# Local attention in one block of 128 scores a head: a predicated fold, a fused maximum and masked parts behind the denominators

## The chip, the cores and the metric

One core of a Trainium2 chip. The metric is the device time of one execution in microseconds (us); the runs shown are medians of three.

The engines: TensorE (PE; its weight loads are PEld), VectorE (DVE), ScalarE (ACT), GpSimd (POOL), SyncE (SP), which here issues the transfers.

## The reference

A decoder block on x (1, 2048, 1024), float32: RMS norm, one input projection, two groups of heads side by side (a gated linear recurrence and sliding-window attention), one output projection, and a SwiGLU network. The change touches the attention:

```python
scores = einsum('bnqhgd,bnshd->bnhgqs', qb, kk) * (B_HEAD_DIM ** -0.5)
dist = qi + BLOCK - kj                       # BLOCK = 128; kj runs over 2 * BLOCK keys: the block before and its own
valid = ((dist >= 0) & (dist < WINDOW))[None] & (key_pos >= 0)[:, None, :]    # WINDOW = 128
scores = scores - slopes[:, :, None, None] * dist
scores = where(valid, scores, -inf)
m = maximum(max(scores, axis=-1), sink)
p = exp(scores - m)
p = p / (sum(p, axis=-1) + exp(sink - m))
o = einsum('bnhgqs,bnshd->bnqhgd', p, vv)
```

There are 8 heads of 64, with 2 heads of keys and values. A query at place q of its block sees the keys q+1 to 127 of the block before and the keys 0 to q of its own: always 128 keys, and each place 0 to 127 is taken exactly once over the two blocks.

## The kernel before

**Blocks and slots.** The 2048 tokens are four blocks of 512 (the loop `for it in range(NSB)`). A block goes through 27 slots. In slots 0 to 21 TensorE makes one group of 128 columns of the input projection (`group`, L940: 24 matmuls, since each f32 product is three of rounded high and low parts), in the later ones parts of the output projection. Between these groups the same slot holds the small steps of attention and of the recurrence, each step of one turn further along. Each engine has its own program with its own loop over the slots, in order, and the engines meet at semaphores. After the four blocks come the two halves of the SwiGLU network (`ffn`, `down`), which the change doesn't touch.

**The weight parts.** For each group, SyncE loads the raw weights, ScalarE makes the high part (`make_hi`, L1251, once the group of the same slot is done), and VectorE the low part (`make_lo`, L1697), two slots ahead of use.

**A turn of attention.** A turn is one pair of heads and 128 queries: 16 turns in a block, 64 in all. The constants SCORE, PROBS, P_TURN and PV (2, 3, 4, 5) say how many slots behind the turn's number a step stands:

- slot i+2: TensorE makes the scores, 256 a head, in bank X[0] (`scores`, L987). VectorE adds the position term from `dist` (or `dist0` where there is no block before), with a large negative number in masked places (L1749, one operation a head), takes the maximum (L1753) and makes two small terms with the sink (L1756, L1760). ScalarE takes the exponentials with their sums (L1332) and that of the sink (L1334).
- slot i+3: VectorE adds up the denominators and takes reciprocals (`denominators`, L1730 and L1734), the first thing in its slot; GpSimd multiplies the probabilities by them (`normalise`, L2300).
- slot i+4: TensorE transposes the four 128x128 parts of `pr` into bank X[1] (`p_turn`, L1010), which must have been read for the turn before (`s_pT`); ScalarE copies the bank to `pT` (`p_turn`, L1340).
- slot i+5: TensorE multiplies by the values, over both blocks of keys (`pv`, L1021).

In VectorE's slot there follow, behind the denominators: `make_lo`, the gate of the recurrence, the low part of the queries (L1884), the scores of turn slot-2, every fourth slot a copy of the outputs (L1892), the recurrence of a head (L1767 to L1793), its mask (L1802), its state update (L1820, eight operations in a row) and its norm (L1828), and the scaling of the block before (L2023). In TensorE's slot the order is group, transposes of the recurrence, scores, `p_turn`, `pv`, and the recurrence's products.

Of the kernel before, what the change touches and what calls it, by code (L numbers as in the profile page):

```python
# [33 lines left out]
F32 = mybir.dt.float32  # L34
# [6 lines left out]
P = 128  # L41
# [86 lines left out]


def step_at(slot, first):  # L130

    return slot - first if 0 <= slot - first < STEPS else None


def block_program(nc, x, ln1_g, w_in, lb_logits, hgrn_norm_g, attn_sinks, attn_norm_g, w_out, ln2_g,
# [37 lines left out]
    with ExitStack() as ctx:  # L173
# [52 lines left out]
        gu = [at(f"gu{i}", (P, T), gu_at + 2 * K * i) for i in range(2)]  # L226
        dist = at("dist", (P, 2 * BLOCK), dist_at)
        dist0 = at("dist0", (P, 2 * BLOCK), dist_at + K)
        causal = at("causal", (P, P), dist_at + 2 * K)
# [190 lines left out]
        s_mx = sem("s_mx")  # L420
        s_nm = sem("s_nm")
        s_nms = sem("s_nms")
        s_exp = sem("s_exp")
        s_den = sem("s_den")
        s_rd = sem("s_rd")
        s_prob = sem("s_prob")
# [12 lines left out]
        s_yblo = sem("s_yblo")  # L439
        s_dist = sem("s_dist")  # L440

# [71 lines left out]

        INI, DST = 10, 4

# [375 lines left out]
        def _(pe):  # L891
# [355 lines left out]
        def _(act):  # L1247
# [147 lines left out]
            def slots(it):  # L1395
                for slot in range(SLOTS):
# [23 lines left out]
                    if slot in Q_SLOT:  # L1420
# [22 lines left out]
                    if slot == SWA_MUL:  # L1443
                        swa_hi(it, 0)
                    for begin, step in ((P_TURN, p_turn), (SCORE, scores), (PV, pv)):
                        i = step_at(slot, begin)
# [225 lines left out]
        def _(dve):  # L1672
            V = nc.vector

            def parameters():
# [18 lines left out]
                V.tensor_copy(causal[:, :].bitcast(I32), causal[:, :]).then_inc(s_ini2, 1)  # L1694
                dve.wait_ge(s_ini2, 11)

# [30 lines left out]
            def denominators(it, i):  # L1727
                w = i % 2
                dve.wait_ge(s_exp, it * STEPS + i + 1)
                V.tensor_tensor(den[:, :], rs[:, w, :], es[:, :], ALU.add).then_inc(s_den, 1)  # L1730
                dve.wait_ge(s_den, it * STEPS + i + 1)
                if i:
                    dve.wait_ge(s_prob, it * STEPS + i)
                V.reciprocal(rd[:, :], den[:, :]).then_inc(s_rd, 1)  # L1734

            def scores(it, i):
# [3 lines left out]
                if i >= 2:  # L1740
                    dve.wait_ge(s_ptr, it * STEPS + i - 1)
                if i == 0 and it:
                    dve.wait_ge(s_dist, it)
                d = dist0 if b == 0 else dist
                for par in range(2):

                    slope = 2.0 ** -(2 * p + par + 1)
                    half = slice(par * 256, (par + 1) * 256)
# [6 lines left out]
                dve.wait_ge(s_mx, it * STEPS + i + 1)  # L1755
                V.scalar_tensor_tensor(out=nm[:, w, :], in0=mx[:, :], scalar=-0.125,  # L1756
                                       in1=nsinks[:, 2 * p:2 * p + 2], op0=ALU.mult,
                                       op1=ALU.min).then_inc(s_nm, 1)
                dve.wait_ge(s_nm, it * STEPS + i + 1)
# [98 lines left out]
            def slots(it):  # L1858
                for slot in range(SLOTS):
                    i = step_at(slot, PROBS)  # L1860
                    if i is not None:
                        denominators(it, i)
                    mul = head_at(slot, NORM_MUL)
                    n = unit_made_at(slot)
# [14 lines left out]
                    if slot in Q_SLOT:  # L1879
                        p = Q_SLOT.index(slot)  # L1880
                        dve.wait_ge(s_qhi, it * PAIRS + p + 1)
                        for par in range(2):
                            rows, others = slice(64 * par, 64 * par + 64), slice(64 - 64 * par, 128 - 64 * par)
                            V.tensor_tensor(qs[p % 2][par][others, :], bank[rows, :],  # L1884
                                            qs[p % 2][par][rows, :].bitcast(F32), ALU.subtract).then_inc(s_q, 1)
# [353 lines left out]
        def _(pool):  # L2239
# [12 lines left out]

            G.iota(dist[:, :].bitcast(I32), [[1, 2 * BLOCK]], base=-BLOCK, channel_multiplier=-1).then_inc(s_ini, 1)
# [4 lines left out]
            G.tensor_copy(dist0[:, :], dist[:, :].bitcast(I32)).then_inc(s_ini, 1)  # L2258
            pool.wait_ge(s_ini, 9)

            G.memset(causal[0:CHUNK, CHUNK:P], 0.0).then_inc(s_ini, 1)

            G.affine_select(out=dist0[:, :], in_=dist0[:, :], compare_op=ALU.is_ge, fill=MASKED, base=BLOCK,
                            pattern=[[-1, 2 * BLOCK]], channel_multiplier=1).then_inc(s_dst, 1)
            pool.wait_ge(s_dst, 1)
            G.affine_select(out=dist[:, :], in_=dist0[:, :], compare_op=ALU.is_ge, fill=MASKED, base=-1,
                            pattern=[[1, 2 * BLOCK]], channel_multiplier=-1).then_inc(s_dst, 1)
            pool.wait_ge(s_dst, 2)
            G.tensor_copy(dist0[:, BLOCK:2 * BLOCK], dist[:, BLOCK:2 * BLOCK]).then_inc(s_dst, 1)
            G.memset(dist0[:, 0:BLOCK], MASKED).then_inc(s_dst, 1)  # L2270
            pool.wait_ge(s_dst, 4)
            pool.wait_ge(s_ini, 10)

# [22 lines left out]
            def normalise(it, i):  # L2296

                pool.wait_ge(s_rd, it * STEPS + i + 1)
                halves = pr[i % 2][:, :].rearrange("p (h k) -> p h k", h=2)
                G.tensor_tensor(halves, halves, rd[:, :].rearrange("p (h o) -> p h o", o=1)  # L2300
                                .broadcast_to([P, 2, 2 * BLOCK]), ALU.mult).then_inc(s_prob, 1)
                if i == (PAIRS - 1) * TB + 1:

                    pool.wait_ge(s_bias, it * STEPS + i)
                    copy(dist0[:, :], dist[:, :]).then_inc(s_dist, 1)

# [99 lines left out]
```

## Time and profile before

| | |
|---|---|
| median of 3 runs | 2208.97 us (2208.25 to 2210.03) |
| the profiled execution | 2210.06 us |
| its span, first to last instruction | 2208.3 us |
| granted TensorE clock, mean | 0.996 |

In the profile's rows, L12 is a line of the kernel; a group is line, engine, operation, output<-inputs by the program's names, count, then busy us, mean ns of one and the idle time of its engine ahead of it with what ended it. Busy time is a union: overlapping instructions count once. Matmuls overlap, so the mean of one is longer than its share. Durations and starts are those of the profiled execution, whose time stands 1.1 us above the median.

### The profile page before, as it was taken

The page shows a single profiled execution, that of the slowest core. Times are in us where ns is not written, and L with a number is a line of the kernel's source. Part 1 is how long each engine was busy: PE and PEld are TensorE (multiplying, and loading weights), DVE is VectorE, ACT ScalarE, POOL GpSimd, SP SyncE. Part 2 cuts the span into 40 slices and gives each one's busy share as a digit, 9 for nine tenths or more (in the row PEclk, how much of TensorE's full clock was granted, in tenths as well). Part 3 has the DMA queues.
Part 4 walks back from the last instruction along what each step waited for, and adds up shares of the span by engine and source line. Part 5 has one row for each costly group of instructions (what it writes and reads, how often), then busy time and mean ns, then how long its engine had stood idle before and what let it go on. Part 6 is the DMA issues. An engine that isn't in the chain of part 4 may idle for free.

```text
span 2208.3 us, 29312 instructions
## 1 busy us (share of the span) xinstructions
PE 2163.4 (98%) x10792; PEld 1788.8 (81%) x10792; DVE 1427.8 (65%) x2126; ACT 972.9 (44%) x1775; POOL 473.4 (21%) x377
## 2 busy tenths in 40 slices
PE   7999999999999999999999999999999999999997
PEld 6887888888888888778888887887888888887886
DVE  5776678657865786857466675568665556454555
ACT  5444454446444644443433333346533333333444
POOL 1342024202320232232232330000223232210000
PEclk9999999999999999999999999999999999999999
DMA  4232332343235324543446566887432323227765
GB/s 125 86 125 68 124 96 87 115 144 104 77 101 166 97 68 139 176 143 121 128 167 220 196 228 210 256 270 253 160 119 90 119 96 119 92 97 238 224 209 214
DMA packets 261534, 323.86 MB, mean 147 GB/s; under 512 B 16400, under 2 KB 167952, under 8 KB 261392
## 3 DMA queue, kind: packets, MB, share of 16 engines
q1 hardware_dynamic: 261392, 321.98, 44.2%
q8 instruction: 87, 1.43, 0.3%
q14 instruction: 55, 0.45, 0.1%
HBM read 244.85 MB, written 77.07 MB: 146 GB/s over the span
## 4 chain that ended last, share of the span: by engine, by line
PE 79%; issue 9%; DVE 5%; POOL 3%; DMA 2%; ACT 1%; SPq 0%; DVEq 0%; POOLq 0%; ACTq 0%
PE M L1194 10%; PE M L1196 10%; PE M L1195 10%; PE M L896 5%; PE M L898 5%; PE M L897 5%; PE M L1220 3%; PE M L1221 3%; PE M L1222 3%; PE X L1196 3%; PE X L1194 3%; PE X L1195 3%; PE X L1220 3%; PE X L1222 3%; PE X L1221 3%
## 5 line engine op out<-in xcount | busy, mean ns | idle before, releaser
L2155 DVE TENSOR_TENSOR ring_lo<-ring_raw,ring_hi 128x1024 fp32r<-128x1024 f32 x154 | 190.6, 1238 | 169.4 <-ACT ring_hi L1604 169.2
L896 PE MATMUL M<-uhi,whi 128*128 128x512 f32 (+1 forms) x720 | 286.1, 397 | 3.7 <-DVE wlo L1701 2.1
L1701 DVE TENSOR_TENSOR wlo<-raw,whi 128x1024 fp32r<-128x1024 f32 x120 | 162.2, 1351 | 196.7 <-ACT whi L1255 196.2
L898 PE MATMUL M<-uhi,wlo 128*128 128x512 f32 (+1 forms) x720 | 278.9, 387 | 0.0
L897 PE MATMUL M<-ulo,whi 128*128 128x512 f32 (+1 forms) x720 | 278.6, 387 | 0.0
L1604 ACT ACTIVATE ring_hi<-ring_raw 128x1024 fp32r<-128x1024 f32 x154 | 163.3, 1061 | 234.6 <-DMA ring_raw<-a_scr 231.1
L1194 PE MATMUL M<-t_hi,wu_hi 128*128 128x512 f32 x616 | 240.7, 391 | 4.4 <-DVE gq L2073 2.6
L1196 PE MATMUL M<-t_hi,wu_lo 128*128 128x512 f32 x616 | 240.4, 390 | 0.0
L1195 PE MATMUL M<-t_lo,wu_hi 128*128 128x512 f32 x616 | 240.1, 390 | 0.0
L1255 ACT ACTIVATE whi<-raw 128x1024 fp32r<-128x1024 f32 x120 | 126.8, 1056 | 207.1 <-PE M L898 129.5
L2041 DVE TENSOR_TENSOR wu_lo<-fraw,wu_hi 128x512 fp32r<-128x512 f32 x132 | 124.9, 955 | 122.5 <-ACT wu_hi L1544 122.1
L2300 POOL TENSOR_TENSOR pr<-pr,rd 128x512 f32<-128x512 f32 x64 | 88.6, 1384 | 459.0 <-DVE rd L1734 459.0
L896 PEld LDWEIGHTS M<-uhi,whi 128*128 128x128 f32 x720 | 136.7, 190 | 35.9 <-issue 7.8
L2369 POOL TENSOR_TENSOR fs<-fraw 128x512 f32<-128x512 f32 x44 | 63.1, 1435 | 456.8 <-DMA fraw<-in_w_gate_dram 210.6
L898 PEld LDWEIGHTS M<-uhi,wlo 128*128 128x128 f32 x720 | 136.5, 190 | 28.1
L897 PEld LDWEIGHTS M<-ulo,whi 128*128 128x128 f32 x720 | 136.8, 190 | 24.4
L1194 PEld LDWEIGHTS M<-t_hi,wu_hi 128*128 128x128 f32 x616 | 115.8, 188 | 29.5 <-DVE wu_lo L2041 4.3
L2375 POOL TENSOR_TENSOR fraw<-fraw,fs 128x512 f32<-128x512 f32 x44 | 58.6, 1332 | 363.2 <-DVE wl_lo L2041 363.2
L1195 PEld LDWEIGHTS M<-t_lo,wu_hi 128*128 128x128 f32 x616 | 116.1, 188 | 24.2
L1196 PEld LDWEIGHTS M<-t_hi,wu_lo 128*128 128x128 f32 x616 | 115.9, 188 | 24.2
L1332 ACT ACTIVATE pr<-pr,nm 128x256 f32<-128x256 f32 x128 | 64.2, 502 | 151.3 <-DVE nms L1760 151.3
L1220 PE MATMUL M<-ring_hi 128*128 128x512 f32 x308 | 120.9, 393 | 4.4 <-DVE ring_lo L2155 4.4
(275 smaller groups left out, 4954.2 us busy)
## 6 DMA issues: line engine op xcount, KB each, us to landing
raw<-in_w_in_dram SPq DMA_DIRECT2D x88, 512.0 KB, 3.9
ring_raw<-a_scr SPq DMA_DIRECT2D x154, 256.0 KB, 3.7
fraw<-in_w_gate_dram SPq DMA_DIRECT2D x44, 512.0 KB, 4.5
fraw<-in_w_up_dram SPq DMA_DIRECT2D x44, 512.0 KB, 4.8
a_scr<-au SPq DMA_DIRECT2D x88, 256.0 KB, 2.4
ring_raw<-t_scr SPq DMA_DIRECT2D x88, 256.0 KB, 3.0
ring_raw<-in_w_down_dram SPq DMA_DIRECT2D x66, 256.0 KB, 3.0
raw<-in_w_out_dram SPq DMA_DIRECT2D x32, 512.0 KB, 3.9
```

The costliest lines, as they stand in the source:

```text
L896: mm(bank, whi[s][:, kb, :], hi, start=first, stop=False)
L897: mm(bank, whi[s][:, kb, :], lo, start=False, stop=False)
L898: return mm(bank, wlo[s][:, kb, :], hi, start=False, stop=last)
L1194: mm(bank[:, :], wh[:, k, :], hi[:, k, :], start=start and k == 0, stop=False, skip_group_check=True)
L1195: mm(bank[:, :], wh[:, k, :], lo[:, k, :], start=False, stop=False, skip_group_check=True)
L1196: last = mm(bank[:, :], wl[:, k, :], hi[:, k, :], start=False, stop=k == KH - 1, skip_group_check=True)
L1220: mm(banks[b][:, :], hi[:, 1, tokens], hi[:, 0, :], start=first, stop=False, skip_group_check=True)
L1221: mm(banks[b][:, :], hi[:, 1, tokens], lo[:, 0, :], start=False, stop=False, skip_group_check=True)
L1222: done = mm(banks[b][:, :], lo[:, 1, tokens], hi[:, 0, :], start=False, stop=last, skip_group_check=True)
L1604: A(hi[:, :, :], raw_r[:, :, :], ACT.Copy).then_inc(s_rowhi, 1)
L1701: V.tensor_tensor(wlo[s][:, :, :], raw[s][:, :, :], whi[s][:, :, :].bitcast(F32), ALU.subtract).then_inc(s_lo[s], 1)
L2155: V.tensor_tensor(lo[:, :, :], raw_r[:, :, :], hi[:, :, :].bitcast(F32), ALU.subtract).then_inc(s_rowlo, 1)
```

## The change

- The scores of a head are folded from 256 to 128 in the bank itself: a predicated copy writes the scores of the own block (places up to q) over those of the block before. The queries are scaled on the way in by 0.125 divided by the head's slope, so that one table `dist` of 128 serves for both blocks.
- One operation a head adds the table, scales and takes the maximum; it takes the place of the addition and the separate maximum. For the first 128 tokens `dist0` has the negative number in the missing places.
- Exponentials and the product with the reciprocals cover 128 a head.
- TensorE transposes two parts a turn in place of four. The two parts (block before, own block) are made by masking with AND as the bank is copied: `p_parts`, on VectorE, in slot i+5 behind the denominators, instead of ScalarE's copy in slot i+4. The product with the values is as before, with its parts in another order.
- GpSimd's set-up makes the new tables; the copy of `dist` once a block goes.

```diff
         dist = at("dist", (P, BLOCK), dist_at)
         dist0 = at("dist0", (P, BLOCK), mix_at + 22 * K)
         upto_row = at("upto_row", (P, BLOCK), dist_at + 512)
         parts = at("parts", (P, 2, BLOCK), dist_at + K)
...
# TensorE, p_turn
-                for n in range(4):
+                for n in range(2):
                     last = tr(X[1][:, n * P:(n + 1) * P], pr[i % 2][:, n * P:(n + 1) * P], ident[:, :])
# TensorE, pv
-                                  pT[i % 2][:, (2 * par + kb) * P:(2 * par + kb + 1) * P],
+                                  pT[i % 2][:, (2 * kb + par) * P:(2 * kb + par + 1) * P],
...
# ScalarE, scores and p_turn
-                    act.wait_ge(s_den, it * STEPS + i)
+                    act.wait_ge(s_den, 2 * (it * STEPS + i) - 1)
                 for par in range(2):
-                    half = pr[w][:, par * 256:(par + 1) * 256]
+                    half = pr[w][:, par * BLOCK:(par + 1) * BLOCK]
...
-            def p_turn(it, i):
-                act.wait_ge(s_ptr, it * STEPS + i + 1)
-                if i >= 2:
-                    act.wait_ge(s_pv, it * STEPS + i - 1)
-                A(pT[i % 2][:, :], X[1][:, :], ACT.Copy).then_inc(s_pT, 1)
...
-                            last = A(qs[p % 2][par][rows, :], bank[rows, :], ACT.Copy)
+                            last = A(qs[p % 2][par][rows, :], bank[rows, :], ACT.Copy, scale=0.125 / slope_of(p, par))
...
# VectorE, scores
-                d = dist0 if b == 0 else dist
+                d = dist0 if it == 0 and b == 0 else dist
+                both = X[0][:, :].rearrange("p (h k) -> p h k", h=2)
+                V.copy_predicated(both[:, :, 0:BLOCK],
+                                  upto_row[:, :].bitcast(I32).rearrange("p (o k) -> p o k", o=1)
+                                  .broadcast_to([P, 2, BLOCK]), both[:, :, BLOCK:2 * BLOCK]).then_inc(s_fold, 1)
+                dve.wait_ge(s_fold, it * STEPS + i + 1)
                 for par in range(2):
-                    last = V.scalar_tensor_tensor(out=pr[w][:, half], in0=d[:, :], scalar=8.0 * slope,
-                                                  in1=X[0][:, half], op0=ALU.mult, op1=ALU.add)
+                    last = V.tensor_tensor_reduce(pr[w][:, par * BLOCK:(par + 1) * BLOCK], both[:, par, 0:BLOCK],
+                                                  d[:, :], 8.0 * slope_of(p, par), MASKED, ALU.add, ALU.max,
+                                                  mx[:, par:par + 1])
                 last.then_inc(s_bias, 1)
                 dve.wait_ge(s_bias, it * STEPS + i + 1)
-                V.tensor_reduce(mx[:, :], pr[w][:, :].rearrange("p (h k) -> p h k", h=2), AX_X,
-                                ALU.max).then_inc(s_mx, 1)
...
+            def p_parts(it, i):
+                dve.wait_ge(s_ptr, it * STEPS + i + 1)
+                if i >= 2:
+                    dve.wait_ge(s_pv, it * STEPS + i - 1)
+                V.tensor_tensor(pT[i % 2][:, :].rearrange("p (k h q) -> p k h q", k=2, h=2).bitcast(I32),
+                                X[1][:, 0:2 * P].rearrange("p (o h q) -> p o h q", o=1, h=2).bitcast(I32)
+                                .broadcast_to([P, 2, 2, P]),
+                                parts[:, :, :].rearrange("p k (o q) -> p k o q", o=1).bitcast(I32)
+                                .broadcast_to([P, 2, 2, P]), ALU.bitwise_and).then_inc(s_pT, 1)
...
# VectorE, slots
                     if i is not None:
                         denominators(it, i)
+                    i = step_at(slot, PV)
+                    if i is not None:
+                        p_parts(it, i)
...
# GpSimd, normalise
-                halves = pr[i % 2][:, :].rearrange("p (h k) -> p h k", h=2)
+                halves = pr[i % 2][:, 0:2 * BLOCK].rearrange("p (h k) -> p h k", h=2)
```

Left out of the diff: the set-up of the tables on GpSimd (some ten small operations in place of six), one cast of `parts` on VectorE, and the low part of the queries, which gets the same scale (`scalar_tensor_tensor` in place of `tensor_tensor`, same shape).

## Rows read from the trace of the kernel before

**Rows 1.** The page's first part: busy us, share, instructions, by engine.

```profile
PE 2163.4 (98%) x10792; PEld 1788.8 (81%) x10792; DVE 1427.8 (65%) x2126; ACT 972.9 (44%) x1775; POOL 473.4 (21%) x377
```

**Rows 2.** Windows: first and second block's attention; length, busy by engine, PEclk, DMA, GB/s.

```profile
39.00:182.00 143.00, 142.37 (x868) 117.79 (x870) 104.82 (x228) 67.38 (x174) 43.02 (x37) 1.00 0.31 100
262.00:406.00 144.00, 142.81 (x876) 117.86 (x874) 110.01 (x232) 76.82 (x188) 42.92 (x37) 1.00 0.29 90
```

**Rows 3.** Groups by line: busy us, mean ns | idle before, releaser.

```profile
L1010 PE MATMUL X<-ident,pr 128*128 128x128 f32 x256 | 38.3, 272 | 0.0
...
L1749 DVE SCALAR_TENSOR_TENSOR pr<-dist,X 128x256 f32<-128x256 f32 x128 | 47.6, 412 | 0.5
L1753 DVE TENSOR_REDUCE mx<-pr 128x2 f32<-128x512 f32 x64 | 43.9, 686 | 2.2
L1820 DVE SCALAR_TENSOR_TENSOR st<-st,cum,X 128x128 f32<-128x128 f32 x112 | 39.0, 348 | 4.0
...
L1802 DVE TENSOR_TENSOR amask<-X,causal 128x512 int32<-128x512 int32 x16 | 10.9, 680 | 0.0
...
L1340 ACT ACTIVATE pT<-X 128x512 f32<-128x512 f32 x64 | 37.8, 590 | 0.2
...
L1332 ACT ACTIVATION_READ_ACCUMULATOR pr<-pr,nm 128x1 f32 x128 | 23.9, 187 | 0.0
...
L2300 POOL TENSOR_TENSOR pr<-pr,rd 128x512 f32<-128x512 f32 x64 | 88.6, 1384 | 459.0 <-DVE rd L1734 459.0
```

**Rows 4.** Timeline of TensorE, second block, turns 1, 5, 7, 10, 11, 12, 15: start, us.

```profile
280.42 0.60 PE L1010 MATMUL X<-ident,pr 128*128 128x128 f32 x4
...
312.03 0.60 PE L1010 MATMUL X<-ident,pr 128*128 128x128 f32 x4
...
329.00 0.60 PE L1010 MATMUL X<-ident,pr 128*128 128x128 f32 x4
...
353.42 0.60 PE L1010 MATMUL X<-ident,pr 128*128 128x128 f32 x4
...
363.81 0.60 PE L1010 MATMUL X<-ident,pr 128*128 128x128 f32 x4
...
371.04 0.60 PE L1010 MATMUL X<-ident,pr 128*128 128x128 f32 x4
...
395.76 0.60 PE L1010 MATMUL X<-ident,pr 128*128 128x128 f32 x4
```

**Rows 5.** Timeline of VectorE, same stretch: reciprocals of turns 2, 6, 8, 11, 12, 13, last update.

```profile
281.05 0.17 DVE L1734 RECIPROCAL rd<-den 128x2 f32<-128x2 f32 x1
...
313.33 0.17 DVE L1734 RECIPROCAL rd<-den 128x2 f32<-128x2 f32 x1
...
329.49 0.17 DVE L1734 RECIPROCAL rd<-den 128x2 f32<-128x2 f32 x1
...
355.36 0.17 DVE L1734 RECIPROCAL rd<-den 128x2 f32<-128x2 f32 x1
...
364.08 0.17 DVE L1734 RECIPROCAL rd<-den 128x2 f32<-128x2 f32 x1
...
372.64 0.17 DVE L1734 RECIPROCAL rd<-den 128x2 f32<-128x2 f32 x1
...
392.95 2.65 DVE L1820 SCALAR_TENSOR_TENSOR st<-st,cum,X 128x128 f32<-128x128 f32 x7
```

**Rows 6.** Timeline of ScalarE and VectorE: the weight parts made ahead of turn 12.

```profile
362.42 1.06 ACT L1255 ACTIVATE whi<-raw 128x1024 fp32r<-128x1024 f32 x1 [1.75 <-PE M L898]
...
364.16 1.22 DVE L1701 TENSOR_TENSOR wlo<-raw,whi 128x1024 fp32r<-128x1024 f32 x1
```

**Rows 7.** Waits of TensorE: who waited for whom, us in total, times, longest.

```profile
PE M L1194 <- DVE gq L2073: 2.6, 1, 2.6
```

**Rows 8.** Windows of the columns of rows 2, in the SwiGLU part.

```profile
942.60:946.00 3.40, 3.40 (x10) 2.63 (x9) 0.18 (x1) 0.59 (x2) 1.00 (x1) 0.50 1.02 337
946.00:949.40 3.40, 3.40 (x16) 2.80 (x15) 0.69 (x1) 1.92 (x5) 0.00 (x0) 0.99 0.61 243
```

More of the change, by code:

```diff
@@ L127, in head_at, with slope_of @@
     return F_SLOT.index(slot - offset) if slot - offset in F_SLOT else None
+def slope_of(p, par):
+    return 2.0 ** -(2 * p + par + 1)
 def step_at(slot, first):
@@ L226, in block_program @@
         gu = [at(f"gu{i}", (P, T), gu_at + 2 * K * i) for i in range(2)]
-        dist = at("dist", (P, 2 * BLOCK), dist_at)
-        dist0 = at("dist0", (P, 2 * BLOCK), dist_at + K)
+        dist = at("dist", (P, BLOCK), dist_at)
+        dist0 = at("dist0", (P, BLOCK), mix_at + 22 * K)
+        upto_row = at("upto_row", (P, BLOCK), dist_at + 512)
+        parts = at("parts", (P, 2, BLOCK), dist_at + K)
         causal = at("causal", (P, P), dist_at + 2 * K)
@@ L420, in block_program @@
         s_mx = sem("s_mx")
-        s_nm = sem("s_nm")
+        s_fold = sem("s_fold")
         s_nms = sem("s_nms")
@@ L1444, in slots @@
                         swa_hi(it, 0)
-                    for begin, step in ((P_TURN, p_turn), (SCORE, scores), (PV, pv)):
+                    for begin, step in ((SCORE, scores), (PV, pv)):
                         i = step_at(slot, begin)
@@ L1694, in parameters @@
                 V.tensor_copy(causal[:, :].bitcast(I32), causal[:, :]).then_inc(s_ini2, 1)
-                dve.wait_ge(s_ini2, 11)
+                V.tensor_copy(parts[:, :, :].bitcast(I32), parts[:, :, :]).then_inc(s_ini2, 1)
+                dve.wait_ge(s_ini2, 12)
             def make_lo(it, n):
@@ L1730, in denominators @@
                 V.tensor_tensor(den[:, :], rs[:, w, :], es[:, :], ALU.add).then_inc(s_den, 1)
-                dve.wait_ge(s_den, it * STEPS + i + 1)
+                dve.wait_ge(s_den, 2 * (it * STEPS + i) + 1)
                 if i:
                     dve.wait_ge(s_prob, it * STEPS + i)
-                V.reciprocal(rd[:, :], den[:, :]).then_inc(s_rd, 1)
+                V.reciprocal(rd[:, :], den[:, :]).then_inc(s_den, 1)
             def scores(it, i):
@@ L1883, in slots @@
                             rows, others = slice(64 * par, 64 * par + 64), slice(64 - 64 * par, 128 - 64 * par)
-                            V.tensor_tensor(qs[p % 2][par][others, :], bank[rows, :],
-                                            qs[p % 2][par][rows, :].bitcast(F32), ALU.subtract).then_inc(s_q, 1)
+                            V.scalar_tensor_tensor(out=qs[p % 2][par][others, :], in0=bank[rows, :],
+                                                   scalar=0.125 / slope_of(p, par),
+                                                   in1=qs[p % 2][par][rows, :].bitcast(F32),
+                                                   op0=ALU.mult, op1=ALU.subtract).then_inc(s_q, 1)
                     i = step_at(slot, SCORE)
@@ L2265, in _ @@
-            pool.wait_ge(s_dst, 1)
-            G.affine_select(out=dist[:, :], in_=dist0[:, :], compare_op=ALU.is_ge, fill=MASKED, base=-1,
-                            pattern=[[1, 2 * BLOCK]], channel_multiplier=-1).then_inc(s_dst, 1)
+            G.iota(upto_row[:, :].bitcast(I32), [[1, BLOCK]], base=-BLOCK, channel_multiplier=-1).then_inc(s_ini, 1)
+            pool.wait_ge(s_ini, 11)
+            G.affine_select(out=dist0[:, :], in_=dist[:, :], compare_op=ALU.is_ge, fill=0.0, base=0,
+                            pattern=[[-1, BLOCK]], channel_multiplier=1).then_inc(s_dst, 1)
@@ L2268, in _ @@
+            G.tensor_copy(parts[:, 1, :], upto_row[:, :].bitcast(I32)).then_inc(s_dst, 1)
             pool.wait_ge(s_dst, 2)
-            G.tensor_copy(dist0[:, BLOCK:2 * BLOCK], dist[:, BLOCK:2 * BLOCK]).then_inc(s_dst, 1)
-            G.memset(dist0[:, 0:BLOCK], MASKED).then_inc(s_dst, 1)
+            G.affine_select(out=parts[:, 1, :], in_=parts[:, 1, :], compare_op=ALU.is_ge, fill=0.0, base=-1,
+                            pattern=[[1, BLOCK]], channel_multiplier=-1).then_inc(s_dst, 1)
+            pool.wait_ge(s_dst, 3)
@@ L2271, in _ @@
+            G.tensor_tensor(dist[:, :], dist0[:, :], parts[:, 1, :], ALU.add).then_inc(s_dst, 1)
             pool.wait_ge(s_dst, 4)
-            pool.wait_ge(s_ini, 10)
+            G.memset(upto_row[:, :], -1.0).then_inc(s_dst, 1)
+            G.memset(parts[:, :, :], -1.0).then_inc(s_dst, 1)
+            G.affine_select(out=dist0[:, :], in_=dist[:, :], compare_op=ALU.is_ge, fill=MASKED, base=0,
+                            pattern=[[-1, BLOCK]], channel_multiplier=1).then_inc(s_dst, 1)
+            pool.wait_ge(s_dst, 7)
@@ new lines, in _ @@
+            G.affine_select(out=upto_row[:, :], in_=upto_row[:, :], compare_op=ALU.is_ge, fill=0.0, base=0,
+                            pattern=[[-1, BLOCK]], channel_multiplier=1).then_inc(s_dst, 1)
+            G.affine_select(out=parts[:, 0, :], in_=parts[:, 0, :], compare_op=ALU.is_ge, fill=0.0, base=-1,
+                            pattern=[[-1, BLOCK]], channel_multiplier=1).then_inc(s_dst, 1)
+            G.affine_select(out=parts[:, 1, :], in_=parts[:, 1, :], compare_op=ALU.is_ge, fill=0.0, base=0,
+                            pattern=[[1, BLOCK]], channel_multiplier=-1).then_inc(s_dst, 1)
@@ L2274, in copy @@
+            pool.wait_ge(s_dst, 10)
             def copy(out, in_):
@@ L2296, in normalise @@
             def normalise(it, i):
-                pool.wait_ge(s_rd, it * STEPS + i + 1)
-                halves = pr[i % 2][:, :].rearrange("p (h k) -> p h k", h=2)
+                pool.wait_ge(s_den, 2 * (it * STEPS + i) + 2)
+                halves = pr[i % 2][:, 0:2 * BLOCK].rearrange("p (h k) -> p h k", h=2)
                 G.tensor_tensor(halves, halves, rd[:, :].rearrange("p (h o) -> p h o", o=1)
[L2301 to L2305, printed above, removed]
+                                .broadcast_to([P, 2, BLOCK]), ALU.mult).then_inc(s_prob, 1)
             def add_squares(it, p):
```

19 lines of the change are left out of this document (5 added, 14 removed).

## The prediction

> **What bounds the kernel now.** I read the busy shares first: TensorE is busy for 98% of the span, VectorE for 65%, ScalarE for 44% [rows 1]. The reader should see that only TensorE is full, so a change pays where it takes work from TensorE and costs where it makes TensorE wait. Then the stretches in which attention runs, one for each block of 512 tokens: in the first TensorE is busy 142.4 of 143 us, in the second 142.8 of 144, and the third and fourth repeat the second within 0.1 us. VectorE is busy 105 and 110 us there, three quarters of the time and far more than its mean [rows 2]. So attention now costs TensorE no waits to speak of, but VectorE is the engine with the least room. Third, the groups of the instructions that the change touches [rows 3], and last the timeline of both engines, turn by turn [rows 4, 5].
>
> A turn i (0 to 15 in a block) is spread over slots: its scores are made in slot i+2, its denominators come at the head of VectorE's slot i+3, TensorE transposes its probabilities in slot i+4 and multiplies by the values in slot i+5. The transposes of turn i share one bank, X[1], with those of turn i-1, and so wait until these are copied out.
>
> **Part 1, two transposes fewer.** Four transposes of 272 ns each [rows 3] take 0.60 us together [rows 4], so they start (0.60 - 0.272) / 3 = 0.109 us apart. Two are left. That is 2 x 0.109 = 0.22 us a turn, 64 turns: 14.0 us of TensorE time, all of it on the path, since TensorE waits for nothing there. The Trainium skill's page TensorE: Matmul & The Clock Gate (section Back-to-back issue gap) has about 81 ns for a sustained 128-column matmul, which would make this 64 x 2 x 0.081 = 10.4 us; the trace's f32 transposes are slower, and the sum goes by the trace.
>
> **Part 2, the copy moves from ScalarE to VectorE, and one slot later.** Now ScalarE copies the bank in 0.59 us [rows 3] in the slot of the transposes, a whole slot before the next ones want it. The changed code makes it an AND of 512 elements on VectorE, at the head of VectorE's next slot, behind the denominators. The nearest row is the causal AND of 128x512 from PSUM, 0.68 us [rows 3]. So the transposes of turn i now wait for this chain: VectorE finishes everything of its slot i+3, makes the sum and reciprocal of turn i+1, then the AND for turn i-1. What is queued behind the wait on TensorE is everything: it runs in order. A VectorE instruction starts 0.09 us before the end shown for the one ahead of it (the reciprocal at 364.08 ends at 364.25, the next starts at 364.16 [rows 5, 6]), and I add 0.06 us for the signal: transposes can start 0.09 less, 0.68 + 0.06 more, so 0.65 us after the reciprocal's end.
>
> Now the reader should set the reciprocal of turn i+1 [rows 5] against the transposes of turn i [rows 4]. In the second block the reciprocal ends after the transposes have started in these turns: turn 1, 281.22 against 280.42, late by 0.80; turn 5, 313.50 against 312.03, 1.47; turn 7, 329.66 against 329.00, 0.66; turn 10, 355.53 against 353.42, 2.11; turn 11, 364.25 against 363.81, 0.44; turn 12, 372.81 against 371.04, 1.77. Today that costs nothing, for nobody on TensorE waits for it. In turn 15 no reciprocal comes ahead, but the state update of VectorE's slot ends at 395.60 and the transposes start at 395.76.
>
> **Part 3, less work in the scores on VectorE.** Gone: two operations of 128x256 at 0.41 us (about 0.74 for the pair, since they overlap) and a maximum over 512 at 0.69 [rows 3]; with the gaps 1.49 us up to the next operation. Added: a predicated copy of 128x256 and two fused operations of 128x128 that also give the maximum. No row shows either form. The copy I take at the 0.41 of a 128x256 operation from PSUM, with the gap 0.45. A 128x128 operation from PSUM is the state update, 0.35 [rows 3]; two that overlap are 0.54, and for writing out the maximum I add 0.1 each, from ScalarE's accumulator read of 0.187 that half overlaps [rows 3]. Together 1.2, a saving of 0.3 us a turn. Bounds: with nothing for the maximum and a cheaper copy, 0.8, saving 0.7; if each of the three takes what 512 elements take, 0.68, it is 2.0, a loss of 0.5. I take 0.3, since the 128x128 row is nearest in size and source. On the maximum the Trainium skill's page VectorE: DVE Perf Modes (Two Vector instructions with no wait between them) says that an operation which also writes out its accumulator is two instructions; no row of VectorE here shows one. With two operations as short as the reciprocal's 0.17 us, unhidden, the saving would be 0.16, and the waits below some 3 us more.
>
> **Part 4, the rest.** ScalarE loses its copy and half of each exponential's elements: it waits for VectorE anyway, so nothing, except that it gives back 0.2 us at turn 1. GpSimd's product goes from 512 to 256 elements (1.38 us for 512 [rows 3]); it runs in the slot ahead of its transposes and waits for VectorE's reciprocal, so nothing. The scaled query copies have the same shapes. The set-up is longer by some small operations on GpSimd and one cast on VectorE, all ahead of the first turn and beside TensorE's first groups: nothing. No DMA is added or moved.
>
> **The sum.** A turn waits for its lateness + 0.65 + 0.22 (TensorE arrives sooner) - 0.3, that is lateness + 0.57. Turn 1: 1.37, less 0.5 because turn 0's saving and the shorter exponentials also come in front of it: 0.9. Turn 5: 2.0. Turn 7: 1.2. Turn 10: 2.7. Turns 11 and 12 need the step back: TensorE stands later by the whole wait, but VectorE stands later only by the AND less its saving, as far as it was behind. At turn 11 that takes 2.7 - 0.3 off, and 0.44 + 0.57 falls under nothing. At turn 12 VectorE began its weight part at 364.16 although ScalarE's half, started at 362.42 and 1.06 long, was there at 363.48 [rows 6]; of the 0.68 it was behind, 0.6 is made good: 1.77 + 0.57 - 0.6 = 1.7. Turn 13 falls under nothing in the same way. Turn 15: 395.60 - 0.09 + 0.68 + 0.06 = 396.25 against 395.54, 0.7. A block: 0.9 + 2.0 + 1.2 + 2.7 + 1.7 + 0.7 = 9.2 us. The first block, where VectorE has 5 us less to do [rows 2], I take at 8. Together 3 x 9.2 + 8 = 36 us.
>
> **The clock.** The attention stretches run at 2.4 GHz [rows 2]. Elsewhere TensorE waited 2.6 us at once [rows 7], and in the 3.4 us from 942.6, soon after it, the granted clock was 0.50, the 1.2 GHz level: 10 matmuls against 16 in the 3.4 us behind [rows 8]. Six lost at 3.4 / 16 = 0.21 us is 1.3 us. Turns 5 and 10 have waits of 2 us or more in all blocks but the first, where only turn 5 has: 7 in all. I count half of these, 5 us, and keep 0 and 10 as bounds.
>
> Net: -14 + 36 + 5 = +27 us. The profiled execution took 2210.06 us with a span of 2208.3; the median of the runs is 2208.97, 1.1 less, so the forecast is about 2236, and I say 2235.
>
> **Rivals.** (A) The waits do not come: VectorE catches up behind the first one, because a late TensorE also gives it time. Then only the transposes count: 2209 - 14 = 2195. For it: at turn 12 it does make 0.6 us good. Against: in most slots VectorE's weight part waits for ScalarE's half, and that for TensorE's group, so a late TensorE delays VectorE as well. Waits of 14 us or less are needed for not slower; with some 20 turns that wait, the saving a turn would have to be 1.2 instead of 0.3, leaving 0.3 us for three operations. 7%. (B) Balance: the saving at its bound 0.7 and half of the waits of turns 5 and 10 made good elsewhere; 36 - 9 - 9 = 18, no clock loss, 2209 + 4 = 2213. 7%. (C) The two fused operations are slow, 0.9 us each: the saving becomes a loss of about 0.8, every waiting turn is 1.1 longer, and turns 2 and 11 join: about +25 more, 2260. For it: they are of a kind that no row shows. 12%. The forecast's own case has 74%.
>
> **How the numbers follow.** Saving 0.7 without clock loss gives 36 - 9 - 14 = +13, 2222; a loss of 0.5 with the full clock cost gives 36 + 18 + 10 - 14 = +50, 2259. Reaching to cases B and C, which lie at these ends, the range is 2213 to 2261; A and what is left over are outside. A measurement can tell 0.2%, 4.4 us, from no change. Faster by more: 7%. Within: 7%. Slower by more: 86%.
>
> **What would show it.** Right: 128 transposes 0.109 us apart; in the list of waits on TensorE, transposes that wait for the AND, 30 to 40 us in some 23 times, longest 2 to 3 us, at turns 1, 5, 7, 10, 12 and 15; the stretches of rows 2 longer by 5 to 7 us each; VectorE's operations up to the small ones 1.2 us a turn; a stretch or two of half clock behind the longest waits. Wrong: no wait of the transposes on VectorE, or TensorE's groups waiting for weight parts instead; a pair of fused operations far from 0.7 us moves the size, not the sign.

## The result, and the profile after

The changed kernel takes 2233.86 us (median of 4 runs, 2228.35 to 2239.69) against 2208.91 for the kernel before: ratio 1.0119, 95% interval 1.0107 to 1.0131. It is slower, by 25 us; the forecast was 2235. The profiled execution took 2233.95 us, its span is 2232.2, so 23.9 us more span than before.

The page's first part, after (before: [rows 1]):

```profile
PE 2160.8 (97%) x10664; PEld 1782.2 (80%) x10664; DVE 1412.5 (63%) x2319; ACT 929.0 (42%) x1711; POOL 419.6 (19%) x380
```

Every engine is busy for less time than before, and the kernel is slower: most of the time went into waits. Where, the windows say (first two blocks' attention, the columns of [rows 2]; they are longer than those by 5 and 8 us):

```profile
39.00:187.00 148.00, 141.48 (x837) 115.68 (x838) 102.49 (x276) 56.21 (x158) 29.00 (x36) 0.99 0.30 97
266.00:418.00 152.00, 143.85 (x857) 117.47 (x856) 107.05 (x281) 67.08 (x173) 28.97 (x36) 0.99 0.28 87
```

TensorE stands still for 6.5 and 8.2 us in them, where it stood for 0.6 and 1.2 before. The groups of the changed lines (busy, mean ns | idle before, releaser; before: [rows 3]):

```profile
L1767 DVE TENSOR_TENSOR pT<-X,parts 128x512 int32<-128x512 int32 x64 | 43.9, 686 | 0.1
L2330 POOL TENSOR_TENSOR pr<-pr,rd 128x256 f32<-128x256 f32 x64 | 39.3, 615 | 506.6 <-DVE rd L1737 506.6
L1752 DVE CUSTOM_DVE_ANT_0 pr<-X,dist 128x128 f32<-128x128 f32 x128 | 32.1, 288 | 2.2
L1747 DVE COPY_PREDICATED X<-upto_row,X 128x256 f32<-128x256 int32 x64 | 26.9, 421 | 0.5
L1018 PE MATMUL X<-ident,pr 128*128 128x128 f32 x128 | 25.6, 283 | 30.6 <-POOL pr L2330 27.3 <-DVE pT L1767 3.0
...
L1752 DVE DVE_READ_ACCUMULATOR2_ANT mx<- 128x1 f32 x128 | 10.6, 83 | 0.0
```

The transposes (L1018) have 30.6 us of idle time in front of them; before, they had none. The profile names GpSimd's product L2330 for 27.3 of it. That name is wrong, and this is worth learning to see. Turn 10 of the second block, TensorE, VectorE and GpSimd:

```profile
359.23 0.64 PE L1005 MATMUL X<-kk,qs 128*128 128x256 f32 x4
362.30 0.41 PE L1018 MATMUL X<-ident,pr 128*128 128x128 f32 x2 [2.42 <-POOL pr L2330]
```

```profile
359.99 1.28 DVE L2040 SCALAR_TENSOR_TENSOR h<-h,rhln,g2row 128x1024 f32<-128x1024 f32 x1
361.19 0.15 DVE L1733 TENSOR_TENSOR den<-rs,es 128x2 f32<-128x2 f32 x1
361.38 0.17 DVE L1737 RECIPROCAL rd<-den 128x2 f32<-128x2 f32 x1
361.46 0.69 DVE L1767 TENSOR_TENSOR pT<-X,parts 128x512 int32<-128x512 int32 x1
```

```profile
349.66 0.61 POOL L2330 TENSOR_TENSOR pr<-pr,rd 128x256 f32<-128x256 f32 x1 [6.61 <-DVE rd L1737]
350.23 1.28 POOL L2338 TENSOR_TENSOR gu<-gu,gu 128x512 f32<-128x512 f32 x1
361.62 0.61 POOL L2330 TENSOR_TENSOR pr<-pr,rd 128x256 f32<-128x256 f32 x1 [10.11 <-DVE rd L1737]
```

The transposes wait for two semaphores. GpSimd's product for this turn ended at 350.27, 12 us before they started. VectorE's AND ended at 362.15, and they started at 362.30. The product that ended at 362.23 is that of turn 11, which they don't need; that the profile names it because its signal came last is my reading, and experiment 4 tests it.

The granted clock, windows around turn 12 of the second block:

```profile
378.70:382.10 3.40, 1.19 (x13) 0.74 (x11) 3.37 (x6) 1.42 (x2) 1.54 (x2) 0.99 0.00 0
382.10:385.50 3.40, 3.40 (x12) 2.64 (x9) 3.30 (x10) 1.49 (x6) 1.05 (x1) 0.50 0.57 170
385.50:388.90 3.40, 3.40 (x17) 2.76 (x16) 1.07 (x4) 0.00 (x0) 2.89 (x4) 1.00 0.74 295
```

Behind the wait of 2.2 us TensorE runs 3.4 us at 1.2 GHz. There are five such stretches in attention (from 91.9, 382.1, 593.7, 614.2 and 846.3 us), none in the attention stretches before. Outside attention, and apart from the last microseconds of the span, each of the two traces has two.

### The profile page after: what moved, and what is told of

It reads as the page before. It is cut to its first block, busy times and chain, and to the rows that moved or that the text cites. A ratio compares the mean times of both kernels' runs of the same rounds, so it can differ in the third digit from the quotient of the medians.

```text
span 2232.2 us, 29183 instructions
## 1 busy us (share of the span) xinstructions
PE 2160.8 (97%) x10664; PEld 1782.2 (80%) x10664; DVE 1412.5 (63%) x2319; ACT 929.0 (42%) x1711; POOL 419.6 (19%) x380
## 4 chain that ended last, share of the span: by engine, by line
PE 71%; issue 14%; DVE 7%; POOL 3%; ACT 2%; DMA 2%; SPq 0%; DVEq 0%; POOLq 0%; ACTq 0%
PE M L1202 9%; PE M L1204 9%; PE M L1203 9%; PE M L1228 3%; PE M L1230 3%; PE M L1229 3%; PE X L1228 3%; PE X L1229 3%; PE X L1230 3%; PE M L903 3%; PE X L1204 3%; PE X L1203 3%; PE X L1202 3%; PE M L905 3%; PE M L904 3%
## 5 line engine op out<-in xcount | busy, mean ns | idle before, releaser
L1704 DVE TENSOR_TENSOR wlo<-raw,whi 128x1024 fp32r<-128x1024 f32 x120 | 151.1, 1259 | 230.6 <-ACT whi L1263 230.4
L2330 POOL TENSOR_TENSOR pr<-pr,rd 128x256 f32<-128x256 f32 x64 | 39.3, 615 | 506.6 <-DVE rd L1737 506.6
L1228 PE MATMUL X<-ring_hi 128*128 128x512 f32 x308 | 120.7, 392 | 0.0
```

What stands on the lines that cost most here:

```text
L1228: mm(banks[b][:, :], hi[:, 1, tokens], hi[:, 0, :], start=first, stop=False, skip_group_check=True)
L1704: V.tensor_tensor(wlo[s][:, :, :], raw[s][:, :, :], whi[s][:, :, :].bitcast(F32), ALU.subtract).then_inc(s_lo[s], 1)
```

## The experiments

**1. The position of the AND.** The same operations, the AND one slot earlier, behind the scores (from here on, edits to the changed kernel unless said otherwise):

```diff
-                    i = step_at(slot, PV)          # head of the slot
-                    if i is not None:
-                        p_parts(it, i)
...
                         scores(it, i)
+                    i = step_at(slot, P_TURN)
+                    if i is not None:
+                        p_parts(it, i)
```

> The changed kernel, with VectorE's AND one slot earlier: behind the scores of the slot in which TensorE makes the transposes, instead of at the head of the next slot. All operations are the same. Theory (the place of the AND makes TensorE wait): the transposes find the bank read a whole slot ahead, the 30.6 us of waits and the half-clock stretches behind them go, and only the 14 us of transposes count: about 2195 us (2192 to 2200), faster than both kernels. Rival (the added VectorE work or the new kinds of operations cost the time wherever they stand, 0.69 us more at the same place in VectorE's order): still over 2220 us, with other waits on VectorE, of TensorE's groups for weight parts for instance.

Measured: 2205.82 us, ratio 0.9988 (0.9978 to 0.9998). The waits of the transposes are gone, so the AND's place was the cause of them. But the forecast of 2195 is missed by 11 us. The waits of TensorE (us in total, times, longest):

```profile
PE X L1054 <- POOL key L2318: 10.5, 8, 2.4
```

Waits for the recurrence's keys have doubled, from 5.3 us before. In turn 13 of three blocks TensorE stands 2.4 us for them, with a half-clock stretch behind two of the waits, and the SwiGLU part has three such stretches where it had one before.

**2. The same with four transposes.**

```diff
-                for n in range(2):
-                    last = tr(X[1][:, n * P:(n + 1) * P], pr[i % 2][:, n * P:(n + 1) * P], ident[:, :])
+                for n in (2, 3, 0, 1):
+                    last = tr(X[1][:, n * P:(n + 1) * P], pr[i % 2][:, n % 2 * P:(n % 2 + 1) * P], ident[:, :])
```

> As the run with the AND one slot earlier, but TensorE makes four transposes a turn (the two of the changed kernel once more into the unused half of the bank). Theory (two transposes fewer are 14.0 us on the path): 14 us above that run, about 2209 us, as the kernel before. Rival (the gain of the earlier AND has another source, and short transposes hide in gaps): within 3 us of that run.

Measured: 2205.74 us, 0.9992 (0.9983 to 1.0001), the same as with two. Read alone, it would say that the saved transposes are worth nothing. The traces say otherwise: from the first transpose to the product behind it are 0.529 us with four and 0.312 with two, and in most turns TensorE falls back by 0.2 us against experiment 1. But the slower TensorE waits for the keys only 5.1 us (7 times, longest 1.0), and behind turn 13 it gets back 1.5, 3.1 and 3.1 us in the last three blocks, the last two with a half-clock stretch spared. So most of what two transposes save comes back as a wait for the keys, which wait for VectorE, and as clock. Experiments 6 and 7 test this.

**3. The position alone, in the kernel before.**

```diff
-            def p_turn(it, i):                     # ScalarE, slot i+4
...
-                A(pT[i % 2][:, :], X[1][:, :], ACT.Copy).then_inc(s_pT, 1)
+            def p_copy(it, i):                     # VectorE, slot i+5, behind the denominators
+                dve.wait_ge(s_ptr, it * STEPS + i + 1)
+                if i >= 2:
+                    dve.wait_ge(s_pv, it * STEPS + i - 1)
+                V.tensor_copy(pT[i % 2][:, :], X[1][:, :]).then_inc(s_pT, 1)
```

> The kernel before with one edit: the copy of the transposed bank is made by VectorE at the head of its next slot, behind the denominators, instead of by ScalarE; 256 scores a head, separate maximum and four transposes stay. Theory: each late turn waits for lateness + 0.65 us with no saving against it: turns 1, 5, 7, 10, 12 and 15 with 1.4, 2.1, 1.3, 2.8, 2.1 and 0.5 us, about 10 us a block and 39 us in all, and 5 to 10 us of clock: about 2255 us (2243 to 2263). Rival (the new kinds of operations or the added set-up are what costs; a copy of 0.68 us is hidden): 2209 to 2215 us.

Measured: 2260.00 us, 1.0231 (1.0214 to 1.0248).

```profile
PE X L1010 <- DVE pT L1760: 39.6, 24, 2.7
```

39 us of waits were expected, 39.6 are there, 24 times, and here the profile names the right engine. No new kind of operation is in this kernel: the move alone makes it some 51 us slower, more than the whole change does, and the change's savings take half of that back.

**4. The order at the head of the slot.** AND first, then the denominators:

```diff
+                    i = step_at(slot, PV)
+                    if i is not None:
+                        p_parts(it, i)
                     i = step_at(slot, PROBS)
                     if i is not None:
                         denominators(it, i)
```

> The changed kernel, with the AND ahead of the denominators at the head of the same VectorE slot. Theory (the transposes wait for VectorE's AND and all in front of it): each of the 23 waits is shorter by the sum and the reciprocal, 0.33 us, so 7 us less in waits, 2226 us (2222 to 2230). Rival (they wait for GpSimd's product, as the profile names it: it comes behind the reciprocals, which now end 0.6 us later): waits as long or longer, 2234 us or above.

Measured: 2227.52 us, 1.0082 (1.0066 to 1.0099), 6 us under the changed kernel, as expected.

```profile
PE X L1018 <- DVE pT L1767: 25.9, 20, 2.1
```

The waits are shorter although the reciprocals, and with them GpSimd's product, come later. In turn 10 of the second block the AND ends at 359.11, the transposes start at 359.25 and GpSimd's product only at 359.45: it is not what they wait for. With its signal later, the profile names the AND.

**5. The clock.** Unused transposes ahead of the waits:

```diff
+                fill = {5: 14, 10: 20 if it else 9, 12: 18 if it else 7}.get(i, 0)
+                if fill:
+                    wait_group_read(pe, it, i + 2)
+                    for n in range(fill):
+                        tr(M[(i + 5) % 3][:, 0:P], pr[i % 2][:, 0:P], ident[:, :])
                 if i:
                     pe.wait_ge(s_pT, it * STEPS + i)
```

> The changed kernel, with unused transposes on TensorE ahead of the wait of turns 5, 10 and 12 (14, 20 and 18 of them, 9 and 7 at the last two in the first block), into the bank of the next group; they take 1.0 to 2.2 us that TensorE would wait, and the result stays the reference's. Theory (the granted clock falls because TensorE stands still there): the waits of these turns shrink below 0.5 us, the turns take no less time, but the five half-clock stretches of 3.4 us in attention go, 1.3 us each: about 2227 us (2225 to 2229), with less spread between runs than the changed kernel's 11 us. Rival (these half-clock stretches have another cause): five or so remain and the time stays at 2234 us or above.

Measured: 2224.58 us (2222.94 to 2227.62), 1.0081 (1.0067 to 1.0095), just under the expected 2225 to 2229. Adding work to TensorE made the kernel 9 us faster. The second block's window at full clock:

```profile
266.00:418.00 152.00, 149.81 (x914) 123.31 (x913) 111.18 (x285) 67.53 (x176) 31.04 (x38) 1.00 0.29 87
```

No half-clock stretch is left in attention, and the spread of the runs fell from 11 to 5 us. So standing still in these waits cost clock. What a stretch costs, the two traces show turn by turn: the step of the transposes from one turn to the next is longer in the changed kernel by 1.5, 1.6, 1.5, 1.5 and 1.5 us where it holds a half-clock stretch, 7.6 us together. The other 1.9 of the 9.5 us between the two at the last turn are not clock: 1.1 are there at the first turn, ahead of any fill, and about 0.1 comes with each filled wait.

**6. The AND behind the recurrence's reciprocals.** Why did experiment 1 wait for keys? In its trace VectorE is in one unbroken run from turn 10 on, the AND at 369.52 stands in front of the reciprocal at 370.73 that the keys need, and GpSimd's product of the keys, which started at 372.61, took 2.34 us instead of 1.3, beside VectorE's weight part. So the AND was put behind `head_group`:

```diff
                     if a is not None:
                         head_group(it, a, part, bank)
+                    i = step_at(slot, P_TURN)
+                    if i is not None:
+                        p_parts(it, i)
                     if mul is not None:
                         head_lo(it, mul)
```

> The AND one slot earlier than in the changed kernel, but behind the reciprocals of the recurrence instead of in front of them. Theory (with the AND right behind the scores, the reciprocals that GpSimd's keys need come 0.69 us later, and TensorE waits 2.4 us for the keys of turn 13 in three blocks, with a half-clock stretch behind two of them): these waits fall to about 1.5 us, the stretches in attention go, no transposes wait: 2201 us (2198 to 2204). Rival (VectorE is behind by all it has done since turn 10, wherever the AND stands): the waits for the keys stay at 2 us or more, and the time within 2 us of 2206.

Measured: 2195.57 us, 0.9942 (0.9922 to 0.9962), better than the expected 2198 to 2204. Run again beside experiment 7:

> The same kernel as the run with the AND one slot earlier behind the reciprocals, for a closer ratio beside the run with four transposes: 0.994 to the kernel before, 2194 to 2197 us.

2194.07 us, 0.9940 (0.9927 to 0.9953). Waits of this run:

```profile
PE X L1054 <- POOL key L2319: 3.0, 4, 1.0
...
PE X L1018 <- DVE pT L1767: 2.1, 6, 0.5
```

The longest wait for keys did not fall to 1.5 us but to 1.0 (1.1 in the first of the two runs), and no half-clock stretch is left before the very end. The AND's place in VectorE's order alone makes 40 us between the changed kernel and this one.

**7. The price of the transposes, where nothing takes their place.** The edit of experiment 2 on experiment 6:

> The fastest kernel so far (the AND one slot earlier, behind the recurrence's reciprocals) with four transposes a turn, two of them made twice. Theory (two transposes fewer are worth 0.217 us a turn, 13.9 us, where nothing takes their place): 2195.6 + 13.9 = 2209.5 us (2206 to 2212). Rival (as the two runs with the AND right behind the scores would have it, the transposes are worth nothing, and this kernel gains by less VectorE work): within 3 us of 2195.6.

Measured: 2206.84 us, 0.9996 (0.9987 to 1.0005), 12.8 us above experiment 6 run beside it, and close to the forecast 13.9. The two traces are less kind to that agreement. At the last turn's transposes they stand 11.5 us apart; 1.2 of that was there at the first turn, and 1.7 came with a half-clock stretch between the first two blocks that the trace with two transposes doesn't have. That leaves some 8.6 us: most turns add 0.2 us, but in turns 6, 7, 11, 12 and 13 nothing is added or some is given back, where the faster TensorE waits a little more (for the AND 2.1 us in all against 0.9, for the recurrence's state 2.7 against 1.9). So two transposes are worth 9 to 13 us here, and nothing like the zero of experiment 2. With four of them the fold, the fused maximum and the AND on VectorE together neither win nor lose.

**8. The masks on GpSimd.** ScalarE copies the two parts in the slot of the transposes, GpSimd masks them in two products of 256:

```diff
+                A(pT[i % 2][:, 0:2 * P], X[1][:, 0:2 * P], ACT.Copy).then_inc(s_pC, 1)      # ScalarE
...
+                pool.wait_ge(s_pC, it * STEPS + i + 1)                                      # GpSimd, end of its slot
+                G.tensor_tensor(own, prev, masks[1], ALU.mult).then_inc(s_pO, 1)
+                pool.wait_ge(s_pO, it * STEPS + i + 1)
+                G.tensor_tensor(prev, prev, masks[0], ALU.mult).then_inc(s_pT, 1)
```

> The changed kernel, with the masked copy taken off VectorE: ScalarE copies the two transposed parts (256 elements) in the slot of the transposes, and GpSimd multiplies them by masks of ones and zeros in two operations at the end of its slot; all other edits of the change stay. Theory (the change gains 14 us of transposes and 0.48 us a turn on VectorE; what it loses is VectorE's AND, by its place or, one slot earlier, by its 0.69 us in front of the reciprocals that GpSimd's keys wait for): no waits of the transposes, waits for the keys 6 us or less as in the kernel before, about 2196 us (2193 to 2200). Rival (two more GpSimd products a turn slow VectorE and the keys): waits for the keys of 10 us or more and over 2203 us.

> As the run with the masks on GpSimd, with four transposes a turn (two of them twice). Theory (two transposes fewer are 14 us on the path where no other wait takes their place; with the AND one slot earlier, waits for the keys and half-clock stretches took it): 14 us above that run, 2208 to 2212 us. Rival (the transposes are worth nothing, as the pair with two and four transposes and the AND one slot earlier seems to say): within 3 us of that run.

Measured: 2259.63 us, 1.0227 (1.0207 to 1.0247), and 2259.95 us, 1.0230 (1.0210 to 1.0251). Both expectations failed: TensorE waits 46.3 us for the masks, 15 times, up to 4.8. Again two transposes made no difference, as they lie in front of a longer wait: with four it is 38.2 us. I took GpSimd's wait for the outputs of the recurrence, ahead of the masks in its slot, for the cause, and moved the masks in front of it:

> The masks on GpSimd as in the run that had them at the end of its slot, now in front of the recurrence's norm factors, for which GpSimd waits until TensorE and ScalarE have made the outputs of the slot. Theory (the 46 us of waits for the masks came from standing behind that wait, not from the work of the two products): waits for the masks fall below 5 us, 2193 to 2200 us. Rival (the two products are too slow or slow VectorE down): 10 us of waits or more remain, over 2205 us.

Measured: 2261.94 us, 1.0244 (1.0229 to 1.0260). This theory fell too. Its waits of TensorE, and GpSimd in the second block's turn 7:

```profile
PE M L1031 <- POOL pT L2333: 44.5, 12, 4.7
```

```profile
349.68 1.54 POOL L2324 TENSOR_TENSOR pr<-pr,rd 128x256 f32<-128x256 f32 x1 [3.10 <-DVE rd L1744]
351.19 1.04 POOL L2309 TENSOR_TENSOR key<-ones,forget 128x512 f32<-128x512 f32 x1
354.25 1.30 POOL L2313 TENSOR_TENSOR key<-key,cuminv 128x512 f32<-128x512 f32 x1 [2.02 <-DVE cuminv L1798]
355.62 1.06 POOL L2316 TENSOR_TENSOR forget<-key,cum 128x512 f32<-128x512 f32 x1
356.64 1.71 POOL L2331 TENSOR_TENSOR pT<-pT,parts 128x256 f32<-128x256 f32 x1
358.43 0.72 POOL L2333 TENSOR_TENSOR pT<-pT,parts 128x256 f32<-128x256 f32 x1
```

The masks (356.64) stand behind the three key operations, and these behind VectorE's reciprocal; ScalarE's copy had been there since 350.19. So they went to the front, between the product with the reciprocals and the keys:

```diff
-                    for offset, step in ((KEY_PRODUCTS, key_steps), (None, p_parts), (NORM_SUM, head_factor),
+                    for offset, step in ((None, p_parts), (KEY_PRODUCTS, key_steps), (NORM_SUM, head_factor),
```

> The masks on GpSimd, now in front of everything but the product with the reciprocals in its slot. The run with the masks in front of the norm factors kept 44.5 us of waits, three a block, each in the slot behind one with the recurrence's keys, in which the masks stood behind the key products and these behind VectorE's reciprocals. Theory (the waits come from standing behind the keys): the masks end 3 us before they are wanted and the keys start as before, since they wait for VectorE's reciprocal anyway: no waits for the masks above 1 us, 2193 to 2200 us. Rival (GpSimd's two products are too much work wherever they stand): waits for masks or keys of 10 us or more, over 2205 us.

Measured: 2191.68 us (2188.94 to 2197.21), 0.9937 (0.9919 to 0.9956), a little under the expected 2193 to 2200. No wait for the masks is left in the list; the keys cost

```profile
PE X L1056 <- POOL key L2313: 4.1, 7, 1.1
```

This kernel and that of experiment 6 beat both the kernel before and the changed one; their intervals overlap, so which of the two is faster stays open. **Not tried:** giving the transposes the two halves of the bank in turn, so that they need not wait for the copy. TensorE would then write one half of the bank while VectorE reads the other; whether that is safe, no run here shows.

## Why the prediction was right

**The bound and the sign.** "Only TensorE is full" and "VectorE is the engine with the least room" hold: the time was lost in waits of TensorE for VectorE, at the turns that the comparison of two timelines named. Experiments 1, 3 and 4 show it from three sides.

**The transposes.** 0.217 us a turn was measured inside the trace (0.529 to 0.312), 13.9 us in all, as forecast; experiment 7 gives 12.8 us of run time. The estimate of 10.4 us, from the 81 ns of the Trainium skill's page TensorE: Matmul & The Clock Gate (section Back-to-back issue gap), would have been too little for the change in step here; the trace's 109 ns decides.

**The waits, turn by turn,** second block, forecast against measured: turn 1, 0.9 and 0.1; turn 5, 2.0 and 1.77; turn 7, 1.2 and 1.01; turn 10, 2.7 and 2.42; turn 12, 1.7 and 2.21; turn 15, 0.7 and 0.64. Sum 9.2 and 8.1. Over four blocks 36 and 30.6. Turns 11 and 13 have none, as forecast. The recorded idle time is not the whole delay. Before, the transposes start 0.17 us ahead of the end shown for the scores in front of them (370.56 + 0.65 against 371.04); behind a longer wait the scores have ended, and this overlap is lost. At each of the 24 waiting turns the transposes come some 0.15 us later than the idle time, less the saved transposes, would have them: 3.6 us in all. From the first transposes of a block to its last, the changed kernel takes 5.4, 6.1, 7.5 and 6.1 us longer, about the 5 to 7 that were forecast.

**Mis-sized: the saving on VectorE.** Taken as 0.3 us with a bound of 0.7; it is 0.48: from the start of the fold (355.72) to the operation behind the maxima (356.73) are 1.01 us, against 1.49. The fold took 0.42 where 0.41 was taken, each fused operation 0.29 where I took the state update's 0.35. The Trainium skill's page VectorE: DVE Perf Modes (Two Vector instructions with no wait between them) is right about the second instruction: each fused operation has an accumulator read behind it, 83 ns, mostly hidden.

**Mis-sized: the chain.** From the reciprocal's end to the transposes I took 0.65 us. It is 0.75 (361.55 to 362.30), since the transposes start 0.15 us behind the AND's end and I had 0.06 for that; no row stood behind the 0.06. With 0.48 and 0.75 the formula gives delays of 1.96, 1.15 and 2.60 us for turns 5, 7 and 10; idle time and the 0.15 together are 1.92, 1.16 and 2.57.

**Missed: waits that TensorE has no longer.** Turn 12 was forecast at 1.7, with a step back of 0.6, and measured 2.21. The rows of turn 11's slot, before, and the same after:

```profile
362.00 0.39 PE L898 MATMUL M<-uhi,wlo 128*128 128x512 f32 x1
362.84 0.66 PE L1084 MATMUL X<-ident,sqo 128*128 128x128 f32 x4 [0.45 <-DVE sqo L1828]
```

```profile
370.73 0.40 PE L905 MATMUL M<-uhi,wlo 128*128 128x512 f32 x1
370.97 0.60 PE L1092 MATMUL X<-ident,sqo 128*128 128x128 f32 x4
372.33 1.23 DVE L1704 TENSOR_TENSOR wlo<-raw,whi 128x1024 fp32r<-128x1024 f32 x1 [1.53 <-ACT whi L1263]
```

The step back came: VectorE's weight part started 2.16 us behind the start of the group's last matmul before (364.16 against 362.00) and starts 1.60 behind it now, where it has waited 1.53 us for ScalarE's half, so 0.56 are made good. But TensorE gained as much. It used to wait there for VectorE's scaled outputs, and their transposes came 0.84 us behind the matmul; now 0.24, so TensorE reaches turn 12 sooner by 0.60. The prediction had put such waits of TensorE at nothing. In all, its waits for the outputs went from 1.3 us to none and those for the keys from 5.3 to 3.0, 3.6 us on the good side.

**Mis-sized: the clock.** Five stretches in attention against a count of half of seven, so 3.5; and a stretch costs 1.5 us (experiment 5) where [rows 8] gave 1.3. Together 7.6 us for the forecast 5.

**The account.** -13.9 (transposes) + 30.6 (idle time) + 3.6 (what the idle time leaves out) + 7.6 (clock) - 3.6 (TensorE's other waits) = +24.3; the last turn's transposes start 24.3 us later (846.7 and 871.0), and the span grew by 23.9. The forecast's -14 + 36 + 5 = +27 had the waits within 2 us, the clock 2.6 too small, and left out the 3.6 of the other waits. Too little saving on VectorE and too short a chain worked against each other, and so did the clock and the other waits. That the total came within 1.2 us of the 2235 (itself 1 below the 2236 of the sum) is luck in part; the sign and the turns are not.

**Rivals.** (A) asked that VectorE catch up; that falls with 24 waits in the trace. Its threshold was also worked out too low: with 20 waiting turns the saving would have to be (36 - 14) / 20 + 0.3 = 1.4 us, not 1.2. But its number, 2195, is what the change gives once the AND stands elsewhere (experiment 6). (B) wanted a saving of 0.7 and no clock loss; it falls with 0.48 and five stretches. (C), slow fused operations, falls with 288 ns.

## What to carry to other kernels

When a copy that frees a buffer moves to another engine, look at its place in that engine's order, which here mattered more than its duration: list, step by step, when the engine reaches that place and when the buffer is wanted, and the lateness plus the new operation is the wait. The same 0.69 us gave +1.2% at the head of a slot, -0.1% in the middle and -0.6% a little further on; as a copy on ScalarE and two products on GpSimd it gave +2.3% and +2.4% or -0.6%, again by its place. Where TensorE is full, an edit that frees it shows its worth only if no queue takes it back, so price it in a variant that has no other waits; and compare turn by turn in the traces what the difference of two medians consists of. Don't trust the releaser's name where an instruction waits for two semaphores, but look up when each was signalled.

## What the runs showed of the hardware

- Ten waits of TensorE in attention lasted 1.77 to 2.42 us; behind five of them stood 3.4 us at 1.2 GHz, behind the others none; with unused transposes in their place there were none in attention, and the kernel ran 9 us faster with more TensorE work. A stretch cost 1.5 us.
- The first transpose behind a wait started 0.15 us after the end of the AND that it waited for, in all 20 of the waits over 0.5 us, and a wait delayed TensorE by some 0.15 us more than its idle time.
- GpSimd's product of 256 elements took 0.61 us, and 1.53 us where VectorE's weight part had started 0.2 us ahead of it (experiments 1 and 4); the keys' product of 512 took 1.3, and 2.34 us where it started with a weight part (experiment 1).
- On VectorE a predicated copy of 128x256 within a PSUM bank took 0.42 us, as much as an addition of that size, and a fused add, scale and maximum of 128x128 0.29 plus a read of 0.08.
